# Five chunks of a depthwise convolution summed by GpSimd, tap by tap, in place of TensorE

## The reference

```python
def conformer_conv_module(h, w_in, b_in, w_dw, b_dw, ln_g, ln_b, w_out, b_out):
    D = h.shape[-1]
    u = h @ w_in + b_in
    u = u[..., :D] * jax.nn.sigmoid(u[..., D:])
    u = lax.conv_general_dilated(
        u, w_dw[:, None, :].astype(u.dtype),
        window_strides=(1,), padding=[(CONV_WIDTH - 1, 0)],
        dimension_numbers=('NWC', 'WIO', 'NWC'), feature_group_count=D) + b_dw
    u = jax.nn.silu(layer_norm(u, ln_g, ln_b))
    return u @ w_out + b_out
```

## Time and profile before

| | |
|---|---|
| median of the runs | 2086.23 us |
| the profiled execution's own time | 2084.2 us |
| its span, first to last instruction | 2082.4 us |
| TensorE matmul busy | 1909.0 us (92%) |
| VectorE busy | 1181.4 us (57%) |
| ScalarE busy | 486.2 us (23%) |
| GpSimd busy | 303.2 us (15%) |
| mean granted TensorE clock | 0.952 of full speed |
| the five calls of `make_taps` on GpSimd (L608) | 10.2 us |

### The profile page before, as it was taken

One profiled execution on the slowest core, in us unless ns is written; L12 is line 12 of the kernel. 1 busy time (PEld: TensorE's weight loads), 2 busy tenths in 40 slices (PEclk: granted clock), 3 DMA queues, 4 the chain that ended last, 5 costly groups with the idle time before them and its releaser, 6 DMA issues.

```text
span 2082.4 us, 49950 instructions
## 1 busy us (share of the span) xinstructions
PE 1909.0 (92%) x19736; PEld 1187.5 (57%) x19736; DVE 1181.4 (57%) x2105; ACT 486.2 (23%) x1027; POOL 303.2 (15%) x464
## 2 busy tenths in 40 slices
PE   5999999999999958999999579999899599999990
PEld 3444444455666635777777357665445467777770
DVE  3547600378899853333333469999995433333336
ACT  3101100456777630000000230010525100000002
POOL 0001030000000012222222400000000222222223
PEclk9999999799999978999999789999999799999995
DMA  9557520100530088777985803033105899854446
GB/s 398 213 202 282 203 62 0 41 11 13 199 134 4 19 310 322 272 293 268 345 332 208 311 30 106 2 114 114 51 0 212 310 408 407 332 216 172 173 173 257
DMA packets 122491, 391.43 MB, mean 188 GB/s; under 512 B 23808, under 2 KB 44928, under 8 KB 118272
## 3 DMA queue, kind: packets, MB, share of 16 engines
q1 hardware_dynamic: 72432, 303.48, 38.3%
q0 software_dynamic: 21904, 66.99, 9.0%
q10 hardware_dynamic: 28032, 19.17, 3.1%
HBM read 337.33 MB, written 47.49 MB: 185 GB/s over the span
## 4 chain that ended last, share of the span: by engine, by line
PE 84%; DVE 8%; DMA 4%; ACT 2%; issue 1%; SPq 0%; POOL 0%; ACTq 0%; DVEq 0%; POOLq 0%
PE ps L1611 24%; PE ps L1621 12%; PE ps L1663 10%; PE ps L1441 9%; PE ps L1496 5%; PE ps L1552 5%; PE ps L1510 4%; PE ps L1523 4%; PE ps L1535 4%; DVE kv L1323 3%; PE ps L1735 3%; DMA kv<-in_w_ada 2%; PE ps L1700 1%; PE ps L1420 1%; DVE pbuf L1015 1%
## 5 line engine op out<-in xcount | busy, mean ns | idle before, releaser
L1611 PE MATMUL ps<-kv,hT 128*32 128x256 f32 x5504 | 386.8, 379 | 2.1 <-DMA kv<-in_w_gate_up 2.1
L1611 PEld LDWEIGHTS ps<-kv,hT 128*32 128x32 f32 x5504 | 241.0, 110 | 64.0 <-issue 2.6
L1323 DVE SCALAR_TENSOR_TENSOR kv<-kv,cols 128x640 f32<-128x640 f32 (+1 forms) x330 | 266.2, 807 | 11.2
L1663 PE MATMUL ps<-hT,ring 128*128 128x320 f32 (+1 forms) x768 | 225.3, 454 | 6.3 <-ACT hT L654 6.3
L1197 DVE TENSOR_TENSOR hT<-hT,modc 128x256 f32<-128x256 f32 x146 | 62.1, 425 | 293.2 <-PE ps L1611 293.1
L1441 PE MATMUL ps<-hT,ring 128*128 128x512 f32 x512 | 221.7, 593 | 1.6 <-ACT hT L654 1.6
L760 ACT ACTIVATE hT<-ps 128x128 f32<-128x128 f32 x146 | 40.5, 277 | 744.3 <-PE ps L1611 744.3
L1028 DVE TENSOR_TENSOR_SCAN pbuf<-hT 128x128 f32<-128x128 f32 (+7 forms) x128 | 173.2, 1353 | 47.3 <-ACT hT L705 47.1
L1663 PEld LDWEIGHTS ps<-hT,ring 128*128 128x128 f32 x768 | 146.2, 192 | 81.9 <-ACT hT L654 6.9
L1441 PEld LDWEIGHTS ps<-hT,ring 128*128 128x128 f32 x512 | 96.7, 190 | 124.8 <-issue 121.9
L1611 PE MATMUL ps<-ring,hT 128*32 128x256 f32 x2560 | 149.8, 385 | 15.9 <-DVE hT L1197 14.3
(11 more groups left out here) (249 smaller groups left out, 2401.1 us busy)
## 6 DMA issues: line engine op xcount, KB each, us to landing
kv<-in_w_gate_up SPq DMA_DIRECT2D x136, 512.0 KB
kv<-in_w_ada SPq DMA_DIRECT2D x21, 2048.0 KB, 7.8
ring<-in_w_gate_up SPq DMA_DIRECT2D x80, 512.0 KB
kv<-in_w_down SPq DMA_DIRECT2D x48, 512.0 KB
ring<-in_w_down SPq DMA_DIRECT2D x40, 512.0 KB
hT<-in_w_gate_up SPq DMA_DIRECT2D x40, 512.0 KB
expert_rows<-hT ACTq DMA_DIRECT2D x584, 32.0 KB
ring<-in_w_in SPq DMA_DIRECT2D x32, 512.0 KB, 11.9
```

What stands on the lines that cost most here:

```text
L1323: ins = V.scalar_tensor_tensor(new, old, w_dw_c[:, c, k:k + 1], new, ALU.mult, ALU.add)
L1611: ins = mm(bank(0)[UNIT * q:UNIT * (q + 1), 0:2 * P], xT[:, c, :], wset[s][q // 2][:, 512 * c + 256 * (q % 2):512 * c + 256 * (q % 2) + 25 ...
L1663: ins = mm(bank((gates_bank, values_bank)[part](i) + b)[:, 0:w], ring[:, j % 3, 512 * k + P * (c % 4):512 * k + P * (c % 4) + P], hT[:, k, ...
```

## The change

The five chunks of `SUMMED` are no longer summed by TensorE. GpSimd multiplies u by one tap into a scratch buffer (`tap_new`, two of them in turn) and adds the scratch to the sum, for each of the 31 taps; the first multiplication takes the bias and writes the sum. The shifted copies, the sets of weights, TensorE's sums and ScalarE's keeping are gone, and with them the waits for them. VectorE's program, `VECTOR`, `GATED_AT` and `TURNED` stay as they were, apart from one small reduction that made a constant for the weights.

```diff
-            for n in range(1, len(SUMMED)):
-                pool.wait_ge(taps_summed, n)
-                make_taps(n)
+            def sum_taps(n):
+                h, c = SUMMED[n]
+                pool.wait_ge(u_done, DC * h + c + 1)
+                if n:
+                    pool.wait_ge(taps_kept, n)
+                for k in range(CW):
+                    old = u_all[:, c, WIDTH[0] * h + k:WIDTH[0] * h + k + WIDTH[h]]
+                    if k == 0:
+                        nc.gpsimd.tensor_scalar(tap_sums[n], old, w_dw_c[:, c, 0:1], b_dw_c[:, c:c + 1], ALU.mult,
+                                                ALU.add).then_inc(tap_added, 1)
+                        continue
+                    if k >= 3:
+                        pool.wait_ge(tap_added, (CW - 1) * n + k - 1)
+                    new = tap_new[k % 2][:, 0:WIDTH[h]]
+                    nc.gpsimd.tensor_scalar(new, old, w_dw_c[:, c, k:k + 1], None, ALU.mult).then_inc(tap_scaled, 1)
+                    if k > 1:
+                        add_tap(n, k - 1)
+                add_tap(n, CW - 1)
+
+            def add_tap(n, k):
+                pool.wait_ge(tap_scaled, (CW - 1) * n + k)
+                pool.wait_ge(tap_added, (CW - 1) * n + k)
+                nc.gpsimd.tensor_tensor(tap_sums[n], tap_sums[n], tap_new[k % 2][:, 0:WIDTH[SUMMED[n][0]]], ALU.add
+                                        ).then_inc(tap_added if k < CW - 1 else taps_kept, 1)
+
+            for n in range(4):
+                sum_taps(n)
             pool.wait_ge(values_done, 2 * DC)
             pool.dma_start(b_gated, b_out.partition_broadcast(P)).then_inc(bc_loaded, 16)
+            sum_taps(4)
...
@@ TensorE
-            def sum_taps(n):
...
             for i in range(1, 2 * DC):
...
                 if i in TURNED_AFTER:
                     turn_chunk(TURNED_AFTER[i])
-                if i in SUMMED_AFTER:
-                    sum_taps(SUMMED_AFTER[i])
             turn_back(0)
             turn_back(1)
-            sum_taps(4)
             project_out(0, 0)
```

More of the change, by code:

```diff
@@ L45 @@
 WIDTH = (P * FIRST, T - P * FIRST)
-TAPS = 4
-TAP_SETS = 8
 SUMMED = [(0, 3), (1, 0), (1, 1), (1, 2), (1, 3)]
@@ L55 @@
 TURNED_AFTER = {2: 0, 4: 1, 6: 2, 7: 3, 8: 4, 10: 5, 12: 6, 14: 7}
-SUMMED_AFTER = {5: 0, 10: 1, 11: 2, 12: 3}
 def trunk(nc, x, c_col, b_ada, final_g, vec_cols, b_out, b_router, w_router, w_ada, w_qkv, w_o, w_in, w_out,
-          w_gate_up, w_down, w_taps, out):
+          w_gate_up, w_down, out):
     f32, i32 = mybir.dt.float32, mybir.dt.int32
@@ L141, in trunk @@
         usig = kv[:, o_:o_ + 2 * WIDTH[0]].rearrange("p (b t) -> p b t", b=2)
-        late_sums = kv[:, o_:o_ + 3 * WIDTH[1]].rearrange("p (b t) -> p b t", t=WIDTH[1])
         pflat = pbuf[:, :, :].rearrange("p b t -> p (b t)")
-        tap_sums = [bcB[:, 0:WIDTH[0]], pflat[:, 1648:1648 + WIDTH[1]]] + [late_sums[:, b, :] for b in range(3)]
-        w_tap = iota_i[:, :].bitcast(f32)
-        fold = maskb[:, :].bitcast(f32)[:, 0:32]
+        tap_sums = ([bcB[:, 0:WIDTH[0]]] + [pflat[:, WIDTH[1] * b:WIDTH[1] * (b + 1)] for b in range(3)]
+                    + [bcA[:, 0:WIDTH[1]]])
+        tap_new = pflat[:, 3 * WIDTH[1]:3 * WIDTH[1] + WIDTH[0]], bcA[:, WIDTH[1]:WIDTH[1] + WIDTH[0]]
         o_ += 2 * WIDTH[0]
@@ L208, in trunk @@
             sem("values_done"), sem("gates_done"), sem("usig_done"), sem("u_done"), sem("conv_done"))
-        conv_turned, conv_kept, diag_made, taps_summed, taps_kept = (
-            sem("conv_turned"), sem("conv_kept"), sem("diag_made"), sem("taps_summed"), sem("taps_kept"))
+        conv_turned, conv_kept, tap_scaled, tap_added, taps_kept = (
+            sem("conv_turned"), sem("conv_kept"), sem("tap_scaled"), sem("tap_added"), sem("taps_kept"))
         ln_root, ln_scaled, bn_made, normed, turned_back, ln_done = (
@@ L213, in trunk @@
             sem("ln_done"))
-        x_biased, shift_loaded = sem("x_biased"), [sem(f"shift_loaded{u}") for u in range(2)]
+        x_biased = sem("x_biased")
         out_done, out_kept, out_read, out_used = sem("out_done"), sem("out_kept"), sem("out_read"), sem("out_used")
@@ L289, in out_bank @@
             return bank((2 if t < FIRST else 6) + half)
[L291 to L303, removed]
         def reduced_after(cc):
@@ L411, in _ @@
             experts(0)
[L412 to L426, removed]
-            for j in range(10):
[L429 to L435, removed]
+            for j in range(10):
                 if j >= 3:
@@ L852, in _ @@
                     keep_chunk(TURNED_AFTER[i])
-                if i in SUMMED_AFTER and SUMMED_AFTER[i] < 2:
-                    keep_taps(SUMMED_AFTER[i])
             def bn_root(g, n):
@@ L871, in _ @@
             activate(1)
-            keep_taps(4)
             normalise(3)
@@ L1723, in project_out @@
                 if n < 2:
-                    if half:
-                        pe.wait_ge(taps_kept, len(SUMMED))
                     pe.wait_ge(cv_loaded[(8 + half) % 3], 16 * PARTS * ((8 + half) // 3 + 1))
@@ L1824, in gate_up @@
         return np.ascontiguousarray(w).reshape(-1, P, DC * 512)
-    shifts = np.pad(a["cv_w_dw"][0][:, :D // 2], ((0, 1), (0, 0))).reshape(TAP_SETS, TAPS, 4, QUARTERS, 32)
     dw = a["cv_w_dw"][0].reshape(CW, DC, P).transpose(2, 1, 0).reshape(P, DC * CW)
@@ L1847 @@
         "w_down": rows(a["moe_w_down"].reshape(-1, QUARTERS, F // P, UNIT, D).transpose(0, 2, 1, 3, 4), F // P),
-        "w_taps": shifts.transpose(1, 4, 2, 3, 0).reshape(P, P),
     }
```

24 lines of the change are left out of this document (removed).

## The result

| | before | after |
|---|---|---|
| median of the runs | 2086.10 us (4 runs, 2084.97 to 2086.30) | 2297.97 us (4 runs, 2296.78 to 2299.17) |
| ratio | | 1.1013, 95% interval 1.0999 to 1.1028 |
| profiled execution's own time, span | 2084.2, 2082.4 us | 2296.8, 2295.0 us |
| GpSimd busy | 303.2 us | 724.0 us |
| mean granted TensorE clock | 0.952 | 0.907 |

A forecast was written before the change was run, and what follows sets the result against it. VectorE's end or the last summed chunk, whichever is later, was taken as the bound: 107.3 us later, plus 7.4 and 2.2 on TensorE, 116.9 on 2084.2 us, 2.0 more for the median: 2203 us, range 2160 to 2260.

The forecast's parts named there:

- What bounds the kernel: From 1290 us TensorE and VectorE are full; the later of VectorE's end and the last summed chunk delays the rest one for one.
- step 6: TensorE behind chunk (1, 3): `turn_chunk(14)` and `project_out(3, 0)` precede `turn_chunk(15)`, 7.4 us more, plus 2.2 us lost to its clock.
- Step 1: Chunk (0, 3), from 1290.3: VectorE loses 36.0 us, the chunk is there at 1382, and TensorE does not wait for it.
- Steps 1, 3 and 4: VectorE's convolution: 36.0 us lost in chunk (0, 3), product 8 at 1414.4, 52.9 us lost after it, end at 1620.0.
- strict alternation at d + 0.54: One 640-column VectorE step per GpSimd instruction of length d, starting d + 0.54 us apart; chance 65%.
- The rival of a port kept over a pair: VectorE gets in only once a tap, behind multiplication and addition, and ends at 1691.8; 2242 us, chance 15%.
- The rival of a harmless one-input instruction: GpSimd's multiplications don't stop VectorE, only additions cost; VectorE ends at 1611.5, 2162 to 2180 us, chance 12%.
- GpSimd's prices: GpSimd's instructions at 640 and 384 columns: additions 1.26 and 0.83 us, multiplications 0.69 and 0.49 us.
- steps 1, 4 and 5: GpSimd's chunks: 59.2 us for chunk (0, 3), 0.657 us an instruction in late ones, chunk (1, 3) there at 1645.6.
- Steps 2 and 7: L608's collisions with VectorE vanish, 1.53 us at 1331 for instance; work taken off TensorE, SP and ScalarE brings nothing.
- step 4: VectorE after product 8: 152.7 us without L608 plus 52.9 us from 191 meetings with GpSimd, ending at 1620.0.

The follow-up runs named there:

- two-operation kernel: The changed kernel with each GpSimd multiplication given a second operation, the addition of 0.0: 2248.27 us, ratio 1.0775 to the kernel before.
- memset kernel: The changed kernel with three GpSimd memsets a tap in place of the multiplication and addition, the five chunks not computed: 2085.53 us.

## Why the prediction was too low

- **What bounds the kernel, and step 6**: right. The end moved with the last summed chunk, and the tail behind it was 10.6 us longer against 9.6. Step 1's "No wait" was wrong: chunk (0, 3) was there at 1420, not 1382, and TensorE waited 20.4 us for it; VectorE, busy for 207 of the next 214 us, had work all the same. The step also puts product 6 at 1403; in the trace before it ends at 1352.4, so that the step's own sum gives 1386.
- **Steps 1, 3 and 4, strict alternation at d + 0.54**: right as a mechanism, exact as a price in the two-operation kernel. In the changed kernel it is not one step to one instruction: a tap at 640 columns has three steps. GpSimd's instructions are longer there by 0.39 and 0.45 us, not by 0.67. The rival of a port kept over a pair is out for the taps, where VectorE gets in after each instruction, though the port was kept over four of them once. The rival of a harmless one-input instruction is half true for the form that the change uses (0.80 of its 1.88 us count), and wrong for the other.
- **The prices ("GpSimd's prices", on which steps 1, 4 and 5 rest)**: here it failed. The forecast named its own test, a 384-column multiplication over 0.83 us, and it took 1.24, above even the upper end. The row that I took for one input was a select at 128 columns, an instruction of another kind; the one for two inputs had broadcast operands.
- **Steps 2 and 7**: right as far as seen. VectorE got some 6 of L608's 7.2 us back in the memset kernel, and TensorE's freed time brought nothing there (2085.53 us).
- **Luck**: the sign was right with the mechanism. That VectorE's end came within 19 us of the forecast (1638.6 against 1620.0) was luck: by the true price of the addition it is 1643.5 or more, but the dear multiplications left GpSimd time for 157 instructions up to then, and not for the 208 of the forecast.

How much each price is worth comes from the prediction's own steps with one price after another replaced.

| | product 8 | VectorE's end | chunk (1, 3) | us |
|---|---|---|---|---|
| as predicted | 1414.4 | 1620.0 | 1645.6 | 2203 |
| additions 1.54 and 0.99 | 1422.8 | 1643.5 | 1672.0 | 2229 |
| multiplications 0.80 and 0.585 as well | 1426.2 | 1656.1 | 1686.3 | 2244 |
| measured in the two-operation kernel | 1426.4 | 1658.4 | 1690.0 | 2248.27 |
| measured in the changed kernel | 1424.3 | 1638.6 | 1740.5 | 2297.97 |

For instance step 4 in the third line: a late chunk has (31 x 0.585 + 30 x 0.99)/61 = 0.784 us a piece, 191 x (0.784 - 0.38) = 77.2, and 1426.2 + 152.7 + 77.2 = 1656.1. Of the 95 us that were missing, 26 are the addition's price and 15 the multiplication's at its cheap form, by these sums; 50 are the one-operation form, by the direct comparison of two kernels; 4 are left over, within the few us by which executions differ here.

In the changed kernel itself the balance is another one, since the dear multiplication uses time of GpSimd that VectorE doesn't lose. By the prices a late tap costs VectorE 0.20 + 0.61 us (0.585 and 0.99 less 0.38 each) and takes GpSimd 2.27 us alone. In the 214.3 us from product 8 to VectorE's end GpSimd makes some 78 of the 124 taps, at 2.73 each; VectorE's end by that is 1424.3 + 152.7 + 78 x 0.81 = 1640. 46 are left and take 46 x 2.27 = 104, measured 101.9 (the third window). The prediction had 36 instructions left there, 18 taps.

Why the one-operation form is slower and gives the port up early is open. It goes with the number of operations asked for, not with the kind of operand (a constant takes 1.17 us at 384, a column 1.24). That it holds the port about as long as the other form fits the rows above; what the engine does in the rest of its time no run shows.

## What to carry to other kernels

- Work moved to GpSimd beside a VectorE that is full with two-input instructions is paid for by VectorE: here on average d - 0.38 us, within 0.1, for each GpSimd instruction that reads and takes d us (0.80 and 0.585 for the dear multiplication, at 640 and 384 columns). Compare that with what VectorE would take to do the work itself. Here a tap cost VectorE 0.81 us at 384 columns by these prices, 61.6/78.5 = 0.78 measured (0.65 if it did the tap itself) and 1.58 at 640 (0.42 for the multiplication, 1.16 for the addition; 0.92 itself), so the move lost before GpSimd's own time was counted.
- Then count GpSimd's time against the window it has: 124 taps of 2.27 us against 157 us. A price that scales from an instruction of another kind or operand pattern is no price; a dozen instructions measured ahead of the program would have settled this one.

## What the runs showed of the hardware

- A GpSimd `tensor_scalar` with one operation takes 2.5 ns a column (1.24, 1.88, 2.85 us at 384, 640, 1024 columns), with a second one 0.84 ns (0.585, 0.80, 1.12). Writing `0.0, mult, add` for `None, mult` took 50 us off a kernel of 2298.
- The dear form keeps a two-input VectorE instruction out for only about 0.8 of its 1.88 us: VectorE's steps beside it were 1.30 and then 0.885 us. Beside a 640-column addition of 1.54 us a step takes 2.04 us, 1.16 more than alone.
- GpSimd's memset, which only writes, disturbs two-input VectorE instructions not at all (210 steps of 640 columns, mean 0.884 us, with memsets of 0.63 us beside them).
- In the taps the two engines alternate when both have a next instruction ready. It is no rule: one step of VectorE took 3.31 us in place of 0.62, over four instructions of GpSimd in a row.
